# Order of TensorE's work in the last attention: scores, values' products and transposes of two heads at a time

## The reference, cut to what matters

```python
def attend(qb):                      # for each block of 128 queries
    s = jnp.einsum('bkgqd,bksd->bkgqs', qb, kh).astype(jnp.float32)
    p = jax.nn.softmax(s, axis=-1).astype(vh.dtype)
    return jnp.einsum('bkgqs,bksd->bkgqd', p, vh)
o = lax.map(attend, q_blocks)        # 2 blocks x 8 heads, 256 keys, head width 64
```

## Time and profile before

| | |
|---|---|
| profiled execution, its own time | 1371.29 us |
| its span | 1369.5 us |
| TensorE busy | 1033.0 us, 75% |
| VectorE busy | 455.4 us, 33% |
| ScalarE busy | 298.4 us, 22% |
| read from HBM | 462.59 MB |
| span of the last attention | about 398.3 to 418.2 us |
| experts | from about 461 us to the end |

### The profile page before, as it was taken

One profiled execution on the slowest core, in us unless ns is written; L12 is line 12 of the kernel. 1 busy time (PEld: TensorE's weight loads), 2 busy tenths in 40 slices (PEclk: granted clock), 3 DMA queues, 4 the chain that ended last, 5 costly groups with the idle time before them and its releaser, 6 DMA issues.

```text
span 1369.5 us, 21789 instructions
## 1 busy us (share of the span) xinstructions
PE 1033.0 (75%) x9296; PEld 666.8 (49%) x9296; DVE 455.4 (33%) x1009; ACT 298.4 (22%) x627; POOL 36.1 (3%) x34
## 2 busy tenths in 40 slices
PE   8999999999999978475665657567566766647565
PEld 6997788878775544242332323234232333324232
DVE  4786785787953422011111101111110111111112
ACT  5654352644731211000100101101000110100000
POOL 0000101011101000000000000000000000000000
PEclk9999999999999999887988979888887988988898
DMA  9562354415575899999999999999999999999996
GB/s 328 155 232 70 133 169 161 156 32 180 181 311 200 332 430 426 423 428 428 423 428 427 425 427 427 425 427 426 426 426 426 426 425 427 427 424 427 427 424 266
DMA packets 71237, 464.35 MB, mean 339 GB/s; under 512 B 6874, under 2 KB 15892, under 8 KB 38548
## 3 DMA queue, kind: packets, MB, share of 16 engines
q1 hardware_dynamic: 69312, 458.90, 82.0%
q10 hardware_dynamic: 1876, 4.75, 1.0%
HBM read 462.59 MB, written 1.05 MB: 339 GB/s over the span
## 4 chain that ended last, share of the span: by engine, by line
DMA 50%; PE 40%; DVE 6%; ACT 1%; SPq 1%; issue 1%; POOL 0%; DVEq 0%; ACTq 0%
DMA ring<-in_w_up 48%; PE bank L1948 15%; PE bank L2425 13%; PE bank L1905 3%; PE bank L1929 2%; DMA ring<-in_w_down 2%; PE bank L1990 2%; PE bank L2020 2%; DVE ring_lo L1215 1%; SPq L584 1%; PE bank L2054 1%; PE bank L2445 1%; DVE qk L1174 1%; DMA res<-in_x 1%; DVE ring_lo L1220 1%
## 5 line engine op out<-in xcount | busy, mean ns | idle before, releaser
L2425 PE MATMUL bank<-ring,expert_area 128*32 128x256 f32 x3840 | 309.9, 489 | 219.1 <-DMA ring<-in_w_up 219.1
L2425 PEld LDWEIGHTS bank<-ring,expert_area 128*32 128x32 f32 x3840 | 143.5, 135 | 378.1 <-DMA ring<-in_w_up 239.0
L1948 PE MATMUL bank<-ring_lo,xt_hi 128*128 128x512 f32 (+3 forms) x576 | 182.9, 386 | 0.6 <-DVE small L1446 0.4
L1792 DVE TENSOR_TENSOR expert_area<-expert_area,bank 128x128 f32<-128x128 f32 x64 | 18.3, 286 | 459.7 <-ACT expert_area L1105 459.7
L1105 ACT ACTIVATE expert_area<-bank 128x128 f32<-128x128 f32 x64 | 17.8, 278 | 609.2 <-PE bank L2425 609.2
L2445 PE MATMUL bank<-ring,consts 128*32 128x256 f32 x1952 | 118.2, 382 | 27.1 <-DVE consts L1794 26.9
L1948 PEld LDWEIGHTS bank<-ring_lo,xt_hi 128*128 128x128 f32 x576 | 104.2, 188 | 20.3 <-issue 3.3
L2445 PEld LDWEIGHTS bank<-ring,consts 128*32 128x32 f32 x1952 | 60.0, 109 | 67.5 <-DVE consts L1794 20.1
L1948 PE MATMUL bank<-ring_lo,xt_lo 128*128 128x512 f32 (+2 forms) x240 | 91.2, 380 | 0.0
L1798 DVE COPY consts<-bank 32x256 f32<-32x256 f32 x63 | 26.5, 421 | 130.8 <-PE bank L2445 130.8
L2514 PE MATMUL bank<-consts,expert_area 128*128 128x512 f32 x120 | 55.1, 602 | 16.2 <-DVE consts L1799 16.2
(11 more groups left out here) (319 smaller groups left out, 1257.2 us busy)
## 6 DMA issues: line engine op xcount, KB each, us to landing
ring<-in_w_down SPq DMA_DIRECT2D x60, 2048.0 KB, 25.0
ring<-in_w_gate SPq DMA_DIRECT2D x59, 2048.0 KB, 18.5
ring<-in_w_up SPq DMA_DIRECT2D x58, 2048.0 KB, 23.1
ring<-in_moba_w_kv SPq DMA_DIRECT2D x4, 2048.0 KB, 8.4
ring<-in_moba_w_in SPq DMA_DIRECT2D x4, 2048.0 KB, 8.2
ring<-in_w_in SPq DMA_DIRECT2D x3, 2048.0 KB, 8.3
ring<-in_mla_w_uq SPq DMA_DIRECT2D x4, 1152.0 KB, 5.9
ring<-in_mla_w_o SPq DMA_DIRECT2D x2, 2048.0 KB, 7.9
```

Of the source, the lines that this page charges most:

```text
L1948: last = nc.tensor.matmul(dst, x[at], w[:, c, :], start=(piece == 0 and c == 0 and w is hi and x is x_hi), stop=(piece == 1 and c == per - ...
L2425: last = nc.tensor.matmul(hidden_in[SLOTS * j:SLOTS * j + SLOTS, :], picked[:, c, SLOTS * i:SLOTS * i + SLOTS], both[:, :, c, j // 2, j % ...
```

## The change

In the last attention, TensorE runs the work of two units together. T and W become the functions `turn` and `weigh`; for kind "g" the loop goes in steps of two, and W of two units and T of two units follow S of two units. Kinds "a" and "b" have the same order as before. The streams of the other engines, all waits, all buffers and all operands are unchanged.

```diff
-                paired = kind == "g"
-                for u in range(units + depth + 1):
-                    if u < units and not (paired and u % 2):
-                        score(u)
-                        if paired:
+                def turn(m):
+                    pe.wait_ge(probs_done, UNIT0[kind] + m + 1)
+                    transposes([probs[:, m % 4, P * k:P * k + P]
+                                for k in range(keys_of(kind, unit_of(kind, m)[1]) // P)])
+                def weigh(m):
+                    h, tile = unit_of(kind, m)
+                    pe.wait_ge(tr_in_sbuf, tr_of_unit(kind, m) + 1)
+                    if m % 8 == 0 and m >= 16:
+                        pe.wait_ge(out_drained, OUT0[kind] + m // 8 - 1)
+                    blocks = keys_of(kind, tile) // P
+                    for k in range(blocks):
+                        last = nc.tensor.matmul(out_bank[m // 8 % 2][:, HD * (h % 8):HD * (h % 8) + HD],
+                                                probs_t[:, m % 2, P * k:P * k + P], values(h, k),
+                                                start=(k == 0), stop=(k == blocks - 1))
+                    if m % 8 == 7:
+                        last.then_inc(out_in_psum, 1)
+                if kind == "g":
+                    for u in range(0, units + 4, 2):
+                        if u < units:
+                            score(u)
                             score(u + 1)
                             if u == 2:
                                 pe.wait_ge(tr_in_sbuf, tr[0] - 1)
                                 nc.tensor.matmul(tr_bank[tr[0] % 2][:], ident, consts[:, 0:512], start=True, stop=True)
+                        if u == units + 2:
+                            beside[18]()
+                        if u >= 4:
+                            weigh(u - 4)
+                            weigh(u - 3)
+                        if 2 <= u < units + 2:
+                            turn(u - 2)
+                            turn(u - 1)
+                    return
...
+                for u in range(units + depth + 1):
+                    if u < units:
+                        score(u)
+                    if 0 <= u - depth < units:
+                        turn(u - depth)
                     if u in beside:
                         beside[u]()
+                    if u - depth - 1 >= 0:
+                        weigh(u - depth - 1)
```

## The result

| | before | after |
|---|---|---|
| median of 15 runs | 1371.83 us (1369.30 to 1373.66) | 1376.07 us (1372.88 to 1377.56) |
| profiled execution, its own time | 1371.29 us | 1374.73 us |
| its span | 1369.5 us | 1372.9 us |

The ratio is 1.0027, with a 95% interval of 1.0021 to 1.0034: slower by 3.7 us, 2.9 to 4.7. (The two medians lie 4.2 us apart; the executions of one kernel scatter over more than 4 us, and the ratio with its interval is the better estimate.) The forecast was 1375.5 us.

The account below looks back on a forecast made before the run. Saturated DMA fills about 462 to 1357 us, but TensorE's last attention decides when it begins. Start +0.45, middle +2.49 and end +1.29 gave +4.23 us on 1371.29: 1375.5 us, own range 1373.6 to 1377.0, with rivals 1372.6 to 1377.4.

Parts of the forecast that it names:

- start, S0 to S4: Start of the last attention: transposes now ahead of the scores wait for the second exponential: +0.45 us.
- middle, S4 to S14: Five steps of 2.62 us plus 0.35 for one longer step: 13.45 us against 10.96, +2.49.
- unit 7's drain: On VectorE the reciprocal and the drain of units 0 to 7 come later, making one step 0.35 us longer.
- end, S14 to mixed transposes: Products and transposes form one line waiting for drains, with no scores to fill it: +1.29 us.
- sum: Start, middle and end of the last attention together: +4.23 us, giving 1375.5 us.
- What bounds: Output projection behind the attention: its delay passes one for one to the saturated DMA stretch and the end.
- The wait: Second product of each step starts 1.59 us after the scores, set by VectorE's queue; step 2.62 us.
- each waits for a drain: At the attention's end, two products and a transpose each wait for a drain; part of the +1.29 us.
- What was costed at nothing: Transfers for experts 1 and 3, issued 3 to 4 us later, cost nothing; without cover, 4 us.
- two covers: For those late transfers: a DMA backlog until about 426 us, then 16 idle us.
- case of a falling clock: Rival: the clock falls in the attention, costing at most 1.75 us more, 1377.2 us; chance 0.05.
- The drains come in time: Rival at each step's second product: no wait, steps of 2.11 us, time 1371.4 to 1372.0 us; chance 0.08.

Follow-up runs that it names:

- the alternating end: W T W T on TensorE at the attention's end: on the changed kernel 1375.46 us; with VectorE also in pairs, ratio 1.0003 to the kernel before, median 1371.85 us.
- the delayed kernel: The kernel before, with ten matmuls on constants added ahead of the output projection; ratio to the kernel before 1.0067 (1.0051 to 1.0082), four executions.

## Why the prediction was right

| term | predicted | measured | what shows it |
|---|---|---|---|
| start, S0 to S4 | +0.45 | 3.41 - 2.96 = +0.45 | 400.38 - 396.97; T1 behind S5 takes 0.31 of it off |
| middle, S4 to S14 | +2.49 | 13.19 - 10.96 = +2.23 | steps 2.57; 2.11 with VectorE in pairs too |
| of it, unit 7's drain | +0.35 | 2.89 - 2.57 = +0.32 | gone with the drain one unit later |
| end, S14 to mixed transposes | +1.29 | 5.18 - 4.05 = +1.13 | 4.01 with the alternating end |
| sum | +4.23 | +3.82 at the projection | ratio 1.0027, 3.7 us |

The terms are confirmed by the distances, not by the time. The median of the changed kernel, 1376.07, lies 0.6 us above the forecast although its attention lost 0.4 less than forecast, and the interval of 2.9 to 4.7 holds 3.82 and 4.23 alike. That 1375.5 came so near is in part luck of the scatter.

*What bounds.* Right: the attention's length decides when the projection starts, and 3.82 us pass to the first expert without loss; the delayed kernel shows the same up to the end with 8.7 us, as far as its interval of 7.0 to 11.2 tells.

*The wait.* The mechanism was right and the size of the step 0.05 too large, 2.62 for 2.57. The term is the start of the second W, 1.59, which is 1.54. I had read D3 at 404.66 as R6's follower. But T3 ends at 404.18 + 0.44 = 404.62, and R6 frees VectorE for the next at 404.28 + 0.34 = 404.62 (0.34 is the distance from R4 to D1 in the changed kernel). D3 waited for both, and started 0.38 behind R6; the 0.04 more was T3's. So the sentence that the second W was "set by S, R, D on VectorE's queue, not by TensorE" holds of the changed kernel and not fully of the one before: there T3 and R6 arrive together. The kernel with VectorE alone in pairs shows it: D3 stands ahead of R6 there, starts 405.11 - 404.00 = 1.11 us after the scores as it does before (404.66 - 403.55), and the step is still 2.18. The change takes T out of this path and leaves R in it. Five steps make about 0.25 of the 0.41 us by which the sum was too high; unit 7's drain, 0.32 for 0.35, adds little.

*The end.* 0.16 too large. The same 0.05 is in its first term: W12 starts 416.51 - 413.57 = 2.94 after S14, not 3.00. And I had let D13 start 0.2 behind the small variance operation and W13 wait for it; W13 follows without an idle piece of its own (one row of eight passes at 416.51), so that "each waits for a drain" was wrong for W13.

*What was costed at nothing.* The transfers for experts 1 and 3 came later by 2.7 us and 3.8 us counted from S0 (414.34 - 396.97 against 413.02 - 398.33, 420.76 - 396.97 against 418.31 - 398.33) and showed in no wait. But of the two covers that the prediction named, the backlog of the DMA engines and the idle time behind it, the first did not hold: with the transfers for experts 1 and 3 issued at 414.34 and 420.76, the engines' share fell to 0.80 and 0.78 between 414 and 418 us and to 0.60 between 422 and 424, where it had been 0.98 to 1.09 before; that the late issues are the cause is read from the times and not tested. What covered the delay was the idle time: the share is 0.00 from 428 to 445 us.

The granted clock stayed at 1.00 in the attention, also with four transposes behind a wait of 0.4 us in every step; so the case of a falling clock, for which the prediction had weighed a rule on transposes from the Trainium skill ("TensorE: Matmul & The Clock Gate", Part 4: PE-mode transpose), did not come.

*The rivals.* "The drains come in time" was not what happened, but its number, 2.11 us a step, was measured when VectorE's order was changed too. The prediction's own range has a slip of 0.1: its bounds add up to 1373.6 to 1376.9.

## What to carry to other kernels

Two engines that hand work to each other through in-order streams have one order between them. Grouping it on one engine alone can put work that used to fill a wait behind the wait: here 0.4 us a step were lost, and with the same grouping on both engines the repeated steps ran without a wait on TensorE. The four combinations of the two orders took 2.18 us a step (neither in pairs), 2.18 (VectorE alone), 2.57 (TensorE alone) and 2.11 (both). Before moving an instruction, write the two streams side by side, and ask of each wait what stands ahead of the awaited instruction on the other engine, and what of one's own now stands behind it.

## What I had not expected

GpSimd, busy 36 us of the whole kernel, can set the end of the attention. The inverse root for tile 0 takes 0.54 us, but stands behind a gating of 1.27 us; it held the scaling for 0.3 us with the alternating end (a start at 416.90, and not at 416.27 + 0.34 = 416.61) and for 0.45 us with VectorE alone in pairs. And the start of the attention scatters by 2.4 us between executions whose code ahead of it is the same (396.97 to 399.35), while distances within it that no edit touches repeat to 0.01 or 0.02 us: a change of 0.3 us can be read there, and not in the time of the kernel.
